# Moving the stationary operands of the split products to 64 bytes past a 128-byte line

## The chip, the cores and the metric

The kernel runs on one core of one Trainium2 chip. The metric is the device time of one execution in microseconds (us); the program is launched once and nothing else runs on the core. A difference of 0.3% is about 3.9 us here.

## What is computed

Four residual layers (a token mixer and a dense MLP each) over one sequence of 256 tokens with 1024 features, all in float32, and a last RMSNorm:

```python
for i in range(DEPTH):                       # DEPTH = 4, mixers: MLA, MoBA, SSD, MLA
    h = rmsnorm(x, norm_mix[i])
    m = mla_mixer(...) | moba_mixer(...) | ssd_mixer(...)
    x = x + m
    x = x + sq_relu_mlp(rmsnorm(x, norm_mlp[i]), mlp_w1[i], mlp_w2[i])
return rmsnorm(x, norm_final)

def sq_relu_mlp(h, w1, w2):                  # w1: 1024 x 4096, w2: 4096 x 1024
    a = jax.nn.relu(h @ w1)
    return (a * a) @ w2
```

The weights are some 220 MB in float32, read from memory once.

## The kernel before, in words

**Products in three parts.** A float32 product is made of three fast ones. Each operand is split into a high part in the type `float32r` and a low part (the rest), and high x high, high x low and low x high are added up in PSUM. `mm3` (L590, L591, L592) does it with 256 or 512 columns; in an MLP the first product is `pe_up` (L982: both halves of the input beside each other, 512 columns; L987: the low weights with 256 columns), and products back to the model width are `pe_out_part` (L902, L903, L906, 512 columns each). Each of these matmuls has its own weight load (LDWEIGHTS) of 128 columns, which is issued ahead, while the matmul before it streams. In the names of the profile's rows the moving operand stands first and the stationary one second: `bank<-hsplit,whi` streams the split input past weights, `bank<-whi,hsplit` and `acc<-whi,uhi` stream weights past a stationary input.

**Weights.** A unit of weights is up to 2048 columns in each of 128 partitions. Units pass through four slots: a DMA from the queue of SP fills `raw`, ScalarE (L557) writes the high part to `whi`, VectorE (L573) writes the rest to `wlo`, and TensorE frees the slot. Units run three ahead of their use. In an MLP a unit of `w1` (`up`) and one of `w2` (`down`) follow each other, 16 of each.

**The input.** The normed input is transposed on TensorE (L795) and split by ScalarE (L646) and VectorE (L723) into `hsplit`, hi and lo halves of 256 tokens for each of 8 feature blocks. Before the change this tensor is used under two layouts: `hsplit`, which begins 16 elements (64 bytes) into a row of 544 elements, in the mixers, and `hflat`, which begins at its first byte with rows of 512, in the MLPs. `split_input(j)` chooses.

**One MLP chunk** (`pe_mlp`, for c of 2 to 15): 24 matmuls of 512 columns for the `down` of two chunks ago, with the squares `uhi`/`ulo` stationary and weights moving; then `pe_up` of this chunk: 16 matmuls of 512 columns (L982) and 16 of 256 (L987), with the weights stationary and `hflat` moving. The mixers' outputs (`ohi`/`olo` of the heads, `ghi`/`glo` of SSD) go through the same `pe_out_part`.

**Order.** All engines' programs are written out by hand; semaphores couple them. PSUM has four accumulators (`acc`) and four banks in turn (`bank`), planned by `Jobs`.

Of the kernel before, what the change touches and what calls it, by code (L numbers as in the profile page):

```python
# [14 lines left out]
F32 = mybir.dt.float32  # L15
F32R = mybir.dt.float32r
# [5 lines left out]
P = 128  # L22
SEQ = 256
# [9 lines left out]
SLOTS = 4  # L33
UNIT = 2048
AHEAD = 3

# [66 lines left out]
def build(nc, A, out, stages):  # L103

    ctx = ExitStack()
    with ctx:
# [98 lines left out]
        with ExitStack() as stage:  # L205
            S_sb = sb("S_sb", [P, 2, 384], F32, stage)
            P_sb = sb("P_sb", [P, 2, 384], F32, stage)
            PT_sb = sb("PT_sb", [P, 2, 384], F32, stage)
            ohi = sb("ohi", [P, 2, 2, SEQ], F32R, stage)
            olo = sb("olo", [P, 2, 2, SEQ], F32R, stage)  # L210
            qT = sb("qT", [P, 2, 4, SEQ], F32, stage)
# [23 lines left out]
        with ExitStack() as stage:  # L235
# [12 lines left out]
            gss = sb("gss", [P, 512], F32, stage)  # L248
            ghi = sb("ghi", [P, 2, 2, SEQ], F32R, stage)
            glo = sb("glo", [P, 2, 2, SEQ], F32R, stage)  # L250
        acs_dram = nc.dram_tensor("acs_rows", (SSD_H, SEQ), F32, kind="Internal").ap()
# [23 lines left out]

        units, first = [], {}

        view = {}

        def unit(key, a, b, *srcs):  # L280

            first[key] = len(units)
            view[key] = (0, a, b)
            units.append((a, b, srcs))

        def unit_of_two(keys, shapes, srcs):

            off, parts = 0, []
            for key, (a, b), src in zip(keys, shapes, srcs):
# [254 lines left out]
        def act_splits(act, key, ahead=AHEAD):  # L544

            while split_to["act"] < min(first.get(key, key) + ahead + 1, len(units)):
# [4 lines left out]
                if k:  # L551
                    act.wait_ge(w_used[s], k)
                lo = 0
                if n in in_halves:
                    lo = e // 2
                    nc.scalar.activation(whi[:, s, :lo], raw[:, s, :lo], ACT.Copy).then_inc(half_hi_done, 1)
                nc.scalar.activation(whi[:, s, lo:e], raw[:, s, lo:e], ACT.Copy).then_inc(w_hi_done[s], 1)  # L557
                split_to["act"] += 1

        def dve_splits(dve, key, ahead=AHEAD):  # L560

            while split_to["dve"] < min(first.get(key, key) + ahead + 1, len(units)):
                n = split_to["dve"]
                s, k = n % SLOTS, n // SLOTS
                e = units[n][0] * units[n][1]
                lo = 0
                if n in in_halves:
                    lo = e // 2
                    dve.wait_ge(half_hi_done, n + 1)
                    nc.vector.tensor_tensor(wlo[:, s, :lo], raw[:, s, :lo], whi[:, s, :lo].bitcast(F32),  # L570
                                            ALU.subtract).then_inc(half_split, 1)
                dve.wait_ge(w_hi_done[s], k + 1)
                nc.vector.tensor_tensor(wlo[:, s, lo:e], raw[:, s, lo:e], whi[:, s, lo:e].bitcast(F32),  # L573
                                        ALU.subtract).then_inc(w_split[s], 1)
# [61 lines left out]

        def split_input(j):

            h = hflat if deferred(j) else hsplit
            return h[:, :, 0, :], h[:, :, 1, :]  # L640

        def act_tr(act, j, t):
            hhi, _ = split_input(j)
            for half in range(2):
# [74 lines left out]
        def dve_tr(dve, j, t, halves=(0, 1)):  # L719
            hhi, hlo = split_input(j)  # L720
            for half in halves:
# [119 lines left out]
        def pe_first_channels(te, j, keys):  # L841
# [5 lines left out]
            half = KD // 2  # L847
            hhi, hlo = split_input(j)

# [124 lines left out]
        def pe_up(te, L, c):  # L974
# [4 lines left out]
            for m in range(2):  # L979
                ps = open_job(te, key + (m,))  # L980
                for k in range(KD):
                    nc.tensor.matmul(ps, w[0][:, k, m * P:(m + 1) * P], hflat[:, k].rearrange("p a n -> p (a n)"),  # L982
                                     start=k == 0, stop=False)
            for m in range(2):
                ps = bank[jobs.at[key + (m,)][0]]
                for k in range(KD):
                    mm = nc.tensor.matmul(ps[:, 0:SEQ], w[1][:, k, m * P:(m + 1) * P], hflat[:, k, 0, :], start=False,  # L987
                                          stop=k == KD - 1)
# [1346 lines left out]
```

## Time and profile before

| | |
|---|---|
| time, median of 3 runs | 1313.64 us (1311.10 to 1315.05) |
| span of the profiled execution | 1312.0 us |
| TensorE busy (matmuls) | 1286.5 us, 98% of the span, 7578 records |
| VectorE, ScalarE busy | 891.4 us (68%), 671.6 us (51%) |
| granted clock of TensorE | 0.998 of 2.4 GHz |
| DMA | 231 MB, 54% of the 16 engines' time |

The span runs from the first to the last instruction of the profiled execution. A matmul's record reaches from its start to the modelled end of its pipeline (390 ns for 512 columns), so records overlap; what a matmul costs is the time from its start to the start of the next one, called its **step** here. It is read from the starts in the timeline: first and last start of a run of matmuls, divided by their number.

### The profile page before, as it was taken

Reading aid. Unit: us, or ns where it says so; the run is one execution under the profiler, and the core shown is the slowest. Engines: PE = TensorE matmul, PEld = TensorE weight load, DVE = VectorE, ACT = ScalarE, POOL = GpSimd, SP = SyncE. Lnnn points to the kernel's source line nnn. Section 1 sums busy time; section 2 is a strip of 40 time slices with the busy share of each in tenths; the row PEclk is TensorE's granted clock in tenths of the full one; section 3 lists DMA queues with packets and bytes.
Section 4 is the critical chain, followed back from the end, with each engine's and each line's share of the span. In section 5 each row is a group of like instructions: output and inputs, shape, how many; then the busy total and the mean of one; then the engine's idle time right before and its main releaser. Section 6 shows DMA issues by size and latency. Waiting matters only on the chain.

```text
span 1312.0 us, 18369 instructions
## 1 busy us (share of the span) xinstructions
PE 1286.5 (98%) x7578; PEld 1126.3 (86%) x7578; DVE 891.4 (68%) x1180; ACT 671.6 (51%) x861; POOL 43.5 (3%) x58
## 2 busy tenths in 40 slices
PE   6999999999999999999999999999999999999998
PEld 5888888888999888887999888888887888888886
DVE  5877666665666666666899886766667876666664
ACT  5555554444555454444776644544445645454442
POOL 3000000000000000000101110000000000000000
PEclk9999999999999999999999999999999999999999
DMA  9744465555845475545574643755554334565540
GB/s 289 143 168 148 141 232 201 193 192 161 233 149 180 132 254 192 192 165 160 181 222 141 203 149 119 249 191 192 191 180 140 117 130 130 168 231 193 192 161 32
DMA packets 146067, 230.93 MB, mean 176 GB/s; under 512 B 7683, under 2 KB 112429, under 8 KB 145984
## 3 DMA queue, kind: packets, MB, share of 16 engines
q1 hardware_dynamic: 143136, 221.66, 50.8%
q0 software_dynamic: 2848, 8.10, 2.9%
q8 instruction: 61, 1.00, 0.3%
q14 instruction: 22, 0.18, 0.0%
HBM read 227.08 MB, written 2.65 MB: 175 GB/s over the span
## 4 chain that ended last, share of the span: by engine, by line
PE 88%; DVE 7%; DMA 1%; issue 1%; ACT 1%; POOL 1%; SPq 0%; POOLq 0%; DVEq 0%; ACTq 0%
PE bank L982 15%; PE acc L902 12%; PE acc L903 12%; PE acc L906 12%; PE bank L987 8%; PE bank L590 7%; PE bank L591 7%; PE bank L592 7%; DVE wlo L573 2%; PE bank L1402 1%; PE bank L1105 1%; PE bank L795 1%; PE bank L1408 1%; PE bank L1090 1%; DMA raw<-in_mla_w_in 1%
## 5 line engine op out<-in xcount | busy, mean ns | idle before, releaser
L573 DVE TENSOR_TENSOR wlo<-raw,whi 128x2048 fp32r<-128x2048 f32 (+2 forms) x207 | 464.7, 2255 | 139.6 <-ACT whi L557 139.5
L557 ACT ACTIVATE whi<-raw 128x2048 fp32r<-128x2048 f32 (+2 forms) x207 | 386.8, 1879 | 45.8 <-PE acc L906 44.2
L982 PE MATMUL bank<-hsplit,whi 128*128 128x512 f32 x896 | 212.2, 389 | 0.0
L903 PE MATMUL acc<-wlo,uhi 128*128 128x512 f32 x512 | 200.1, 391 | 0.0
L902 PE MATMUL acc<-whi,uhi 128*128 128x512 f32 x512 | 199.6, 390 | 0.0
L982 PEld LDWEIGHTS bank<-hsplit,whi 128*128 128x128 f32 x896 | 168.2, 188 | 34.9
L906 PE MATMUL acc<-whi,ulo 128*128 128x512 f32 x512 | 159.2, 390 | 0.0
L590 PE MATMUL bank<-hsplit,whi 128*128 128x256 f32 (+2 forms) x540 | 154.5, 286 | 0.3 <-DVE xn L1980 0.3
L592 PE MATMUL bank<-hsplit,wlo 128*128 128x256 f32 (+2 forms) x540 | 151.4, 280 | 0.0
L591 PE MATMUL bank<-hsplit,whi 128*128 128x256 f32 (+2 forms) x540 | 151.4, 280 | 0.0
L1027 ACT ACTIVATE relu<-bank 128x512 f32<-128x512 f32 x56 | 33.5, 598 | 188.9 <-PE bank L987 188.9
L987 PEld LDWEIGHTS bank<-hsplit,wlo 128*128 128x128 f32 x896 | 114.9, 191 | 4.4
L987 PE MATMUL bank<-hsplit,wlo 128*128 128x256 f32 x896 | 116.2, 283 | 0.0
L906 PEld LDWEIGHTS acc<-whi,ulo 128*128 128x128 f32 x512 | 96.1, 188 | 20.4
L903 PEld LDWEIGHTS acc<-wlo,uhi 128*128 128x128 f32 x512 | 96.4, 188 | 18.2
L902 PEld LDWEIGHTS acc<-whi,uhi 128*128 128x128 f32 x512 | 96.4, 188 | 18.0
L1048 DVE TENSOR_TENSOR relu<-bank,relu 128x512 f32<-128x512 f32 x56 | 38.7, 691 | 96.0 <-ACT relu L1027 96.0
L590 PEld LDWEIGHTS bank<-hsplit,whi 128*128 128x128 f32 (+2 forms) x540 | 100.9, 187 | 1.7 <-issue 1.3
L591 PEld LDWEIGHTS bank<-hsplit,whi 128*128 128x128 f32 (+2 forms) x540 | 100.8, 187 | 0.9 <-issue 0.7
L592 PEld LDWEIGHTS bank<-hsplit,wlo 128*128 128x128 f32 (+2 forms) x540 | 100.7, 187 | 0.0
L1032 ACT ACTIVATE uhi<-rsq 128x512 fp32r<-128x512 f32 x64 | 40.5, 633 | 110.6 <-DVE rsq L1050 81.9
L1053 DVE TENSOR_TENSOR ulo<-rsq,uhi 128x512 fp32r<-128x512 f32 x64 | 44.3, 693 | 47.6 <-ACT uhi L1032 47.6
(252 smaller groups left out, 1813.4 us busy)
## 6 DMA issues: line engine op xcount, KB each, us to landing
raw<-in_mlp_w SPq DMA_DIRECT2D x128, 1024.0 KB, 5.5
raw<-in_ssd_w_in SPq DMA_DIRECT2D x18, 1024.0 KB, 5.4
raw<-in_mla_w_o SPq DMA_DIRECT2D x16, 1024.0 KB, 4.9
raw<-in_mla_w_ukv SPq DMA_DIRECT2D x8, 1024.0 KB, 5.8
raw<-in_moba_w_qkv SPq DMA_DIRECT2D x16, 512.0 KB, 5.3
raw<-in_ssd_w_out SPq DMA_DIRECT2D x8, 1024.0 KB, 4.9
raw<-in_mla_w_uq SPq DMA_DIRECT2D x8, 768.0 KB, 6.0
raw<-in_mla_w_in SPq DMA_DIRECT2D x4, 1024.0 KB, 7.5
```

What stands on the lines that cost most here:

```text
L557: nc.scalar.activation(whi[:, s, lo:e], raw[:, s, lo:e], ACT.Copy).then_inc(w_hi_done[s], 1)
L573: nc.vector.tensor_tensor(wlo[:, s, lo:e], raw[:, s, lo:e], whi[:, s, lo:e].bitcast(F32), ALU.subtract).then_inc(w_split[s], 1)
L590: nc.tensor.matmul(ps, lhs[0], rhs[0], start=start, stop=False)
L591: nc.tensor.matmul(ps, lhs[0], rhs[1], start=False, stop=False)
L592: return nc.tensor.matmul(ps, lhs[1], rhs[0], start=False, stop=stop)
L902: nc.tensor.matmul(acc[t][half][:], lh, wh[:, k, n], start=begin and k == 0, stop=False)
L903: nc.tensor.matmul(acc[t][half][:], lh, wl[:, k, n], start=False, stop=False)
L906: mm = nc.tensor.matmul(acc[t][half][:], ll, wh[:, k, n], start=False, stop=end and k == 1)
L982: nc.tensor.matmul(ps, w[0][:, k, m * P:(m + 1) * P], hflat[:, k].rearrange("p a n -> p (a n)"), start=k == 0, stop=False)
L987: mm = nc.tensor.matmul(ps[:, 0:SEQ], w[1][:, k, m * P:(m + 1) * P], hflat[:, k, 0, :], start=False, stop=k == KD - 1)
L1032: nc.scalar.activation(uhi[:, c % 2].rearrange("p a b -> p (a b)"), rsq[:, c % 2, :], ACT.Copy).then_inc(uhi_done, 1)
L1053: nc.vector.tensor_tensor(ulo[:, c % 2].rearrange("p a b -> p (a b)"), rsq[:, c % 2, :], uhi[:, c % 2].rearrange("p a b -> p (a b)").bitca ...
```

## The change

It moves addresses within the partitions, and nothing else: each engine issues the same instructions, with the same sizes and waits, in the same order. Where the operands of the three-part products start, in bytes modulo 128, in the programs as they are built:

| moving, stationary | matmuls | before | after |
|---|---|---|---|
| L982: `hsplit`, `whi` (512 columns) | 896 | 0, 0 | 0, 64 |
| L987: `hsplit`, `wlo` (256) | 896 | 0, 0 | 0, 64 |
| L902, L903, L906: `whi`/`wlo`, `uhi`/`ulo` (512) | 1536 | 0, 0 | 0, 64 |
| the same with `ohi`/`olo`, `ghi`/`glo` (512) | 672 | 0, 0 | 0, 64 |
| L590 to L592, L855 to L861: `hsplit`, weights, first two chunks of an MLP (256) | 384 | 0, 0 | 0, 64 |
| L590 to L592: `hsplit`, weights, in mixers (256) | 1248 | 64, 0 | 0, 64 |
| L590 to L592: `chi`/`clo`, weights of `uq` (256) | 192 | 0, 0 | 0, 64 |
| L590 to L592: weights of `mv`, `hsplit` (256) | 180 | 0, 64 | 64, 0 |
| L590 to L592, L1312 to L1318: weights of `ca`/`cb`, `hsplit` (512) | 84 | 0, 64 | 0, 0 |

`uq` is MLA's query weights, `mv` MoBA's value weights, `ca`/`cb` MLA's input weights. Each slot of `whi` and `wlo` grows by 128 bytes, to 8320, so that slots start in turn at 128 and 0 modulo 256. `hflat` and `split_input` go, and `hsplit` is one dense tensor at a 128-byte line.

```diff
+HALF_LINE = 16
-        whi = sb("whi", [P, SLOTS, UNIT], F32R)
-        wlo = sb("wlo", [P, SLOTS, UNIT], F32R)
+        whi = sb("whi", [P, SLOTS, UNIT + 2 * HALF_LINE], F32R)
+        wlo = sb("wlo", [P, SLOTS, UNIT + 2 * HALF_LINE], F32R)
-        hrows = sb("hsplit", [P, KD, 2 * SEQ + 32], F32R)
-        hsplit = hrows[:, :, 16:16 + 2 * SEQ].rearrange("p k (a n) -> p k a n", a=2)
-        hflat = hrows[:].rearrange("p k n -> p (k n)")[:, 0:KD * 2 * SEQ].rearrange("p (k a n) -> p k a n", k=KD, a=2)
+        hsplit = sb("hsplit", [P, KD, 2, SEQ], F32R)
-            uhi = sb("uhi", [P, 2, 2, SEQ], F32R, stage)
-            ulo = sb("ulo", [P, 2, 2, SEQ], F32R, stage)
+            uhi, ulo = (sb(n, [P, 2 * HALF_LINE + 4 * SEQ], F32R, stage)[:, HALF_LINE:-HALF_LINE].rearrange(
+                "p (b a n) -> p b a n", b=2, a=2) for n in ("uhi", "ulo"))
...
+        def start_of(kind):
+
+            if kind in ("ca", "cb", "down", "wo", "so", "ukv"):
+                return (0, 0)
+            return (HALF_LINE, HALF_LINE) if kind == "up" else (HALF_LINE, HALF_LINE)
+
         def unit(key, a, b, *srcs):
 
             first[key] = len(units)
+            starts.append(start_of(key if key == "dt" else key[0]))
...
             off, a, b = view[key]
             s = first[key] % SLOTS
-            return (whi[:, s, off:off + a * b].rearrange("p (a b) -> p a b", a=a),
-                    wlo[:, s, off:off + a * b].rearrange("p (a b) -> p a b", a=a))
+            hi, lo = (off + start for start in starts[first[key]])
+            return (whi[:, s, hi:hi + a * b].rearrange("p (a b) -> p a b", a=a),
+                    wlo[:, s, lo:lo + a * b].rearrange("p (a b) -> p a b", a=a))
...
-        def split_input(j):
-
-            h = hflat if deferred(j) else hsplit
-            return h[:, :, 0, :], h[:, :, 1, :]
-
...
                 for k in range(KD):
-                    nc.tensor.matmul(ps, w[0][:, k, m * P:(m + 1) * P], hflat[:, k].rearrange("p a n -> p (a n)"),
+                    nc.tensor.matmul(ps, w[0][:, k, m * P:(m + 1) * P], hsplit[:, k].rearrange("p a n -> p (a n)"),
                                      start=k == 0, stop=False)
```

`ohi`/`olo` and `ghi`/`glo` change as `uhi`/`ulo` do, and the splits on ScalarE and VectorE (L557, L573) write to the shifted places.

## Rows read from the trace of the kernel before

**Rows 1.** Page, parts 1 and 2: busy time by engine; granted clock in tenths
```profile
PE 1286.5 (98%) x7578; PEld 1126.3 (86%) x7578; DVE 891.4 (68%) x1180; ACT 671.6 (51%) x861; POOL 43.5 (3%) x58
PEclk9999999999999999999999999999999999999999
```

**Rows 2.** Page, part 4: the chain that ended last, by engine
```profile
PE 88%; DVE 7%; DMA 1%; issue 1%; ACT 1%; POOL 1%; SPq 0%; POOLq 0%; DVEq 0%; ACTq 0%
```

**Rows 3.** Waits of TensorE and VectorE: total us, times, longest us
```profile
PE bank L795 <- DVE xn L700: 8.9, 2, 8.0
PE acc L902 <- DVE wlo L573: 0.8, 2, 0.4
...
DVE wlo L573 <- ACT whi L557: 139.5, 136, 3.4
```

**Rows 4.** Timeline of TensorE, one MLP chunk: start us, us, engine, line
```profile
302.81 0.40 PE L902 MATMUL acc<-whi,uhi 128*128 128x512 f32 x1
...
308.28 3.79 PE L982 MATMUL bank<-hsplit,whi 128*128 128x512 f32 x16
311.91 2.08 PE L987 MATMUL bank<-hsplit,wlo 128*128 128x256 f32 x16
...
313.82 0.40 PE L902 MATMUL acc<-whi,uhi 128*128 128x512 f32 x1
```

**Rows 5.** Timeline, weights of `ca`/`cb` streaming past `hsplit`, fourth layer and first
```profile
992.28 0.40 PE L591 MATMUL bank<-wlo,hsplit 128*128 128x512 f32 x1
992.52 0.39 PE L592 MATMUL bank<-whi,hsplit 128*128 128x512 f32 x1
992.75 0.40 PE L590 MATMUL bank<-whi,hsplit 128*128 128x512 f32 x1
...
1000.41 0.28 PE L590 MATMUL bank<-hsplit,whi 128*64 128x256 f32 x1
...
26.16 0.40 PE L591 MATMUL bank<-wlo,hsplit 128*128 128x512 f32 x1
...
28.72 0.33 PE L590 MATMUL bank<-hsplit,whi 128*64 128x256 f32 x1
```

**Rows 6.** Timeline, weights of `mv` streaming past `hsplit` in MoBA
```profile
343.35 0.28 PE L592 MATMUL bank<-whi,hsplit 128*128 128x256 f32 x1
...
346.07 0.28 PE L592 MATMUL bank<-whi,hsplit 128*128 128x256 f32 x1
```

**Rows 7.** Timeline, `hsplit` streaming past weights in SSD, a mixer
```profile
648.83 0.28 PE L590 MATMUL bank<-hsplit,whi 128*128 128x256 f32 x1
...
652.01 0.28 PE L590 MATMUL bank<-hsplit,whi 128*128 128x256 f32 x1
```

**Rows 8.** Timeline, `hsplit` streaming past weights in an MLP's first two chunks
```profile
161.75 0.28 PE L590 MATMUL bank<-hsplit,whi 128*128 128x256 f32 x1
...
166.31 0.28 PE L592 MATMUL bank<-hsplit,wlo 128*128 128x256 f32 x1
```

**Rows 9.** Timeline, one step of a mixer's output product among attention's matmuls
```profile
138.57 0.39 PE L903 MATMUL acc<-wlo,ohi 128*128 128x512 f32 x1
...
141.11 0.59 PE L1105 MATMUL bank<-PT_sb,v_sb 128*128 128x256 f32 x2
141.54 0.27 PE L1106 MATMUL bank<-PT_sb,v_sb 128*128 128x128 f32 x1
```

**Rows 10.** Windows: us, then busy (instructions) of PE, PEld, DVE, ACT, POOL; PEclk, DMA share, GB/s
```profile
302.82:313.82 11.00, 11.00 (x58) 9.42 (x57) 6.66 (x5) 4.96 (x4) 0.00 (x0) 1.00 0.56 186
992.28:1000.41 8.13, 8.13 (x37) 6.52 (x35) 6.16 (x6) 6.54 (x9) 0.70 (x1) 1.00 0.28 79
343.35:346.07 2.72, 2.72 (x27) 2.72 (x25) 1.72 (x2) 2.72 (x2) 0.00 (x0) 1.00 1.04 355
```

**Rows 11.** The line of VectorE's half of the input split: min/median/max ns, forms
```profile
L723 DVE TENSOR_TENSOR hsplit<-bank,hsplit x32: 679/688/693, 9.7 to 1132.0; 128x512 fp32r<-128x512 f32 x32
```

More of the change, by code:

```diff
@@ L208, in build @@
             PT_sb = sb("PT_sb", [P, 2, 384], F32, stage)
-            ohi = sb("ohi", [P, 2, 2, SEQ], F32R, stage)
-            olo = sb("olo", [P, 2, 2, SEQ], F32R, stage)
+            ohi, olo = (sb(n, [P, 2 * HALF_LINE + 4 * SEQ], F32R, stage)[:, HALF_LINE:-HALF_LINE].rearrange(
+                "p (b a n) -> p b a n", b=2, a=2) for n in ("ohi", "olo"))
             qT = sb("qT", [P, 2, 4, SEQ], F32, stage)
@@ L248, in build @@
             gss = sb("gss", [P, 512], F32, stage)
-            ghi = sb("ghi", [P, 2, 2, SEQ], F32R, stage)
-            glo = sb("glo", [P, 2, 2, SEQ], F32R, stage)
+            ghi, glo = (sb(n, [P, 2 * HALF_LINE + 4 * SEQ], F32R, stage)[:, HALF_LINE:-HALF_LINE].rearrange(
+                "p (b a n) -> p b a n", b=2, a=2) for n in ("ghi", "glo"))
         acs_dram = nc.dram_tensor("acs_rows", (SSD_H, SEQ), F32, kind="Internal").ap()
@@ L276, in build @@
         units, first = [], {}
+        starts = []
         view = {}
+        def start_of(kind):
+            if kind in ("ca", "cb", "down", "wo", "so", "ukv"):
+                return (0, 0)
+            return (HALF_LINE, HALF_LINE) if kind == "up" else (HALF_LINE, HALF_LINE)
         def unit(key, a, b, *srcs):
             first[key] = len(units)
+            starts.append(start_of(key if key == "dt" else key[0]))
             view[key] = (0, a, b)
@@ L288, in unit_of_two @@
             off, parts = 0, []
+            starts.append(start_of(keys[0][0]))
             for key, (a, b), src in zip(keys, shapes, srcs):
@@ L552, in act_splits @@
                     act.wait_ge(w_used[s], k)
-                lo = 0
+                lo, high = 0, whi[:, s, starts[n][0]:starts[n][0] + e]
                 if n in in_halves:
                     lo = e // 2
-                    nc.scalar.activation(whi[:, s, :lo], raw[:, s, :lo], ACT.Copy).then_inc(half_hi_done, 1)
-                nc.scalar.activation(whi[:, s, lo:e], raw[:, s, lo:e], ACT.Copy).then_inc(w_hi_done[s], 1)
+                    nc.scalar.activation(high[:, :lo], raw[:, s, :lo], ACT.Copy).then_inc(half_hi_done, 1)
+                nc.scalar.activation(high[:, lo:e], raw[:, s, lo:e], ACT.Copy).then_inc(w_hi_done[s], 1)
                 split_to["act"] += 1
@@ L565, in dve_splits @@
                 e = units[n][0] * units[n][1]
-                lo = 0
+                lo, high, low = 0, whi[:, s, starts[n][0]:starts[n][0] + e], wlo[:, s, starts[n][1]:starts[n][1] + e]
                 if n in in_halves:
@@ L569, in dve_splits @@
                     dve.wait_ge(half_hi_done, n + 1)
-                    nc.vector.tensor_tensor(wlo[:, s, :lo], raw[:, s, :lo], whi[:, s, :lo].bitcast(F32),
+                    nc.vector.tensor_tensor(low[:, :lo], raw[:, s, :lo], high[:, :lo].bitcast(F32),
                                             ALU.subtract).then_inc(half_split, 1)
                 dve.wait_ge(w_hi_done[s], k + 1)
-                nc.vector.tensor_tensor(wlo[:, s, lo:e], raw[:, s, lo:e], whi[:, s, lo:e].bitcast(F32),
+                nc.vector.tensor_tensor(low[:, lo:e], raw[:, s, lo:e], high[:, lo:e].bitcast(F32),
                                         ALU.subtract).then_inc(w_split[s], 1)
@@ L719, in dve_tr @@
         def dve_tr(dve, j, t, halves=(0, 1)):
-            hhi, hlo = split_input(j)
             for half in halves:
@@ L986, in pe_up @@
                 for k in range(KD):
-                    mm = nc.tensor.matmul(ps[:, 0:SEQ], w[1][:, k, m * P:(m + 1) * P], hflat[:, k, 0, :], start=False,
+                    mm = nc.tensor.matmul(ps[:, 0:SEQ], w[1][:, k, m * P:(m + 1) * P], hsplit[:, k, 0, :], start=False,
                                           stop=k == KD - 1)
```

2 lines of the change are left out of this document (removed).

## The prediction, made before the run

> **What bounds the kernel now.** I read the busy shares first: TensorE has work in flight for 98% of the span, at a granted clock of nine tenths or more in every slice; VectorE is at 68%, ScalarE at 51% [rows 1]. The chain that ended last is 88% TensorE [rows 2], and TensorE waits for little: 8.9 us in all for the normed input, 0.8 us for split weights [rows 3]. VectorE waits 139.5 us for ScalarE's half of the weight split, so the splitting engines have slack. The end is set by TensorE's own steps, and what counts is how long a matmul of 256 or 512 columns holds the engine until the next may start.
>
> So the next view is the timeline, read for steps. At 2.4 GHz, 512 columns stream in 213.3 ns and 256 in 106.7 ns. One MLP chunk [rows 4]: 24 `down` matmuls from 302.81 to 308.28 us are 227.9 ns each; the 16 of L982 from 308.28 to 311.91 are 226.9; the 16 of L987 from 311.91 to 313.82 are 119.4. The clock in that window is 1.00 of full [rows 10], so 13 ns a matmul are neither the stream nor a slow clock. Since VectorE is busy for only 6.66 of these 11.00 us and TensorE never pauses, it is not a wait for another engine either. What runs beside a stream is the next weight load.
>
> **What alignment does, as far as this trace shows it.** The trace of before holds three of the four combinations of (moving, stationary) modulo 128:
> - (0, 0): the MLP chunk, 227 ns and 119.4 ns [rows 4]; with 256 columns also the first two chunks of an MLP, 38 steps from 161.75 to 166.31 us, 120.0 ns each [rows 8].
> - (64, 0), 256 columns: the mixers' products, 27 steps from 648.83 to 652.01 us, 117.8 ns [rows 7].
> - (0, 64), which the change makes the rule. 256 columns: MoBA's `mv`, 24 steps from 343.35 to 346.07, 113.3 ns [rows 6]. 512 columns: MLA's `ca`/`cb` in the fourth layer, 35 steps from 992.28 to 1000.41, 232.3 ns, and in the first, 11 steps from 26.16 to 28.72, 232.7 ns [rows 5].
>
> So the same shift shortens a 256-column step by 6 ns and lengthens a 512-column step by 5. The 512-column steps were not slowed by waits: no row of the stretch has one, and the clock is 1.00 [rows 10]. Nor do they settle: 232.3 is a mean over steps that move around it (240 and 230 are the first two [rows 5]), where the 512-column steps of the MLP stand still at 226.9. I read it so: with 256 columns the weight load (128 columns at half the rate) is as long as the stream and sets the step, and a load from a shifted place isn't held up; with 512 columns the load is over in half the step, and it is the stream that pays for the meeting, a little more when the two lie 64 bytes apart.
>
> The Trainium skill speaks against any effect at all. By its page "SBUF — State Buffer", section "Who interferes with whom", TensorE has two independent read ports, one for the moving operand and one for LDWEIGHTS, and never waits on anyone; by that rule the sum would be 0. The steps above, which differ by 6.7 ns with nothing but the address changed, do not agree with it.
>
> **The sum**, against the span of 1312.0 us; the median of the runs is 1.6 us above it:
> - L982, 896 x (232.3 - 226.9) = +4.8 us.
> - `down` of the MLPs, 1536 matmuls from 227.9 to 232.3: +6.8 us.
> - `wo` and `so`, 672 matmuls. Among attention's matmuls they come in short runs whose steps are already 230.9 ns (11 from 138.57 to 141.11 us [rows 9]), in long ones as in the MLP: between 672 x 1.4 = +0.9 and 672 x 4.4 = +3.0; I take +2.0, the middle, as the trace has both kinds.
> - L987, 896 x (113.3 - 119.4) = -5.5 us.
> - First two chunks of the MLPs, 384 x (113.3 - 120.0) = -2.6 us.
> - Mixers' products, 1248 x (113.3 - 117.8) = -5.6 us; the first step behind a wait is not shortened, and I take -5.0.
> - `uq`'s 192 with `chi`, which is (0, 0) now: -1.3 us.
> - `mv`, the other way round: 180 x (117.8 - 113.3) = +0.8 us. `ca`/`cb` go to (0, 0): 84 x (227 - 232.3) = -0.4 us.
> - The splits and evictions write 64 bytes off. L723 does so before the change in the mixers and not in the MLPs, and takes 679 to 693 ns over both [rows 11]: 0, and what it took would be hidden behind TensorE's work. In the mixers TensorE gets 4% faster; the weights come three units ahead and waited-for splits are 0.8 us [rows 3], so I let nothing new become late.
>
> The three terms of 512 columns give +13.6 us, those of 256 give -13.6, `ca`/`cb` -0.4: **-0.4 us**, a span of 1311.6 and a time of 1313.64 - 0.4 = 1313.2, call it 1313.5 for the stretches where a step beside a wait keeps its length. It is a small difference of two large terms: 1 ns in the step of the 3104 wide matmuls is 3.1 us. The samples of that step are 46, in two layers; 231 to 233.5 is as far as I trust them, which is -4 to +4 us.
>
> **Rivals.**
> 1. *The wide steps stay as they are.* In every wide run of before, the step becomes steady at 226.9. The samples of (0, 64) alternate between stationary tiles at 64 and 192 modulo 256 from one feature block to the next; in L982 after the change, a whole run keeps one of them, and could settle. Then only the narrow terms are left: -14 us, 1299.7 us. Against it: within the samples, three matmuls in a row with the same place don't settle. Half of it (L982 alone, or only some slots) would be 1305 to 1309.
> 2. *The streams meet no load any more.* If 64 bytes apart were the cure in wide products too, the step would come near the stream. The nearest row is the float32 product of L1105, two records of 215 ns [rows 9]: 3104 x (215 - 227.6) = -39 us on top of -14, 1261 us. The samples at 232 speak against it. The Trainium skill ("TensorE: Matmul & The Clock Gate", section "Back-to-back issue gap") gives 518 cycles at N=512 and 262 at N=256, an estimate of 216 and 109 ns; by it all steps of before are 6 to 10 ns too long, and the sum would be some -36 us for the wide ones alone. No stretch of fast products in this trace reaches those.
> 3. *Slower: a steady slow step.* The same settling, but at a longer step. The wide products after the change see streams at 128 and at 0 modulo 256 (slots of 8320 bytes), the samples only 128. The first steps in the samples reach 240 ns; at a steady 236 the wide terms are +26 us against -14, so 1325.5 us. It decides from 233.6 ns on: 3104 x 1.3 ns is the 3.9 us that make 0.3%.
> 4. *The addresses don't matter*, and the differences come from what else goes on in those stretches. Then the time is 1313.6. The 256-column steps of 113.3 with DMA at 1.04 of its engines and both splitters at work [rows 10] speak against it; it isn't told apart from my forecast by the time, but by the steps.
>
> **How the numbers follow.** My forecast (wide 231 to 233.5, narrow 113.3) gets 0.50, rival 1 with its halves 0.23, rival 2 0.06, rival 3 0.17, rival 4 0.04. A change within 0.3% (3.9 us) is about what a measurement of this kernel can't tell from none. Same: nearly all of the forecast (0.43) and rival 4, with 0.02 from light forms of the others: 0.49. Faster: rivals 1 and 2, and the forecast's low end: 0.32. Slower: rival 3 and the high end: 0.19. The range has to take in rival 1 whole (1299.7, with 2 us for the bounds of its narrow terms: 1297.5) and most of rival 3 (to a wide step of 234.7, 1321); outside are rival 2 and the worst of rival 3, some 0.12, and a little at both ends. The forecast's own range is 1309.5 to 1317.5.
>
> **What the profile after would show.** Right: L987's 16 steps in 1.81 us instead of 1.91, and the mixers' steps at 113.3 in place of 117.8, while L982's 16 take 3.72 us instead of 3.63 and do not stand still; the chunk stays at about 11.0 us. Wrong, to the fast side: L982's 16 in 3.63 us or less. Wrong, to the slow side: a wide step above 233.6, most likely in the slots that start at 0 modulo 256, or a wait of TensorE for `wlo` in the mixers, where VectorE is now asked for units 4% sooner. What would upset the whole working is a narrow step that isn't 113.3 outside MoBA: the only samples of it have the input stationary and the weights moving, and the change has it the other way round.

## The result, and the profile after

The kernel after takes 1322.53 us, the median of 4 runs (1318.5 to 1323.55); the kernel before took 1314.35 us beside it (1311.1 to 1315.71). The ratio is 1.0063, 95% interval [1.0043, 1.0083]. The change makes the kernel slower by some 8 us. The forecast was no change (1313.5 us), and the measured time lies above the range's upper end of 1321.0. Two of ten executions of u_up_shifted (1424.17 and 5673.52 us) and one of the kernel before beside the last two experiments (1363.52 us) ran over 1.5% above the fastest of their kernel and are left out of all comparisons.

The page of one execution of the kernel after, which took 1318.5 us, the fastest of the four; parts 1, 2 and 4:

```profile
span 1316.7 us, 18369 instructions
PE 1289.6 (98%) x7578; PEld 1116.2 (85%) x7578; DVE 891.2 (68%) x1180; ACT 672.0 (51%) x861; POOL 43.5 (3%) x58
PEclk9999999999999999999999999999999999999999
PE 84%; DVE 11%; ACT 2%; issue 1%; DMA 1%; POOL 0%; SPq 0%; POOLq 0%; DVEq 0%; ACTq 0%
```

Little here looks different from [rows 1]: the same instructions, the same busy shares, the same clock. TensorE's busy time is 3.1 us longer. The chain is still TensorE's, 84% where it was 88% [rows 2], with VectorE at 11% where it was 7%. Waits are few, as in [rows 3], with one that is new, the first `down` product of each MLP for VectorE's squares:

```profile
PE bank L797 <- DVE xn L703: 8.6, 2, 7.5
PE acc L903 <- DVE ulo L1054: 0.9, 4, 0.2
PE acc L903 <- DVE wlo L582: 0.8, 2, 0.4
DVE wlo L582 <- ACT whi L566: 144.4, 136, 3.4
```

So the loss must be in the steps. The timeline of TensorE in the kernel after, read as [rows 4] was, one MLP chunk of the first MLP and one of the third (start us, us, engine, line; L983 is what was L982, L988 was L987, L903 was L902):

```profile
177.91 3.83 PE L983 MATMUL bank<-hsplit,whi 128*128 128x512 f32 x16
181.57 1.98 PE L988 MATMUL bank<-hsplit,wlo 128*128 128x256 f32 x16
183.38 0.39 PE L903 MATMUL acc<-whi,uhi 128*128 128x512 f32 x1
...
188.97 3.83 PE L983 MATMUL bank<-hsplit,whi 128*128 128x512 f32 x16
...
850.14 3.89 PE L983 MATMUL bank<-hsplit,whi 128*128 128x512 f32 x16
853.88 1.98 PE L988 MATMUL bank<-hsplit,wlo 128*128 128x256 f32 x16
855.70 0.40 PE L903 MATMUL acc<-whi,uhi 128*128 128x512 f32 x1
...
861.25 3.90 PE L983 MATMUL bank<-hsplit,whi 128*128 128x512 f32 x16
```

In the first MLP L983 steps at 3.66 / 16 = 229 ns (the single steps go round 232, 226 and 229) and L988 at 1.81 / 16 = 113 ns; in the third at 3.74 / 16 = 234 and 1.82 / 16 = 114 ns. `down` takes 5.59 / 24 = 233 ns there and 5.55 / 24 = 231 here. The chunk, 11.01 us before, is 11.06 and 11.11 us. The clock is not in it; the window view of both chunks (us; busy of PE, PEld, DVE, ACT, POOL; PEclk, DMA share, GB/s) has it at 1.00, as in [rows 10]:

```profile
177.91:188.97 11.06, 11.06 (x58) 9.33 (x57) 7.70 (x7) 7.03 (x6) 0.00 (x0) 1.00 0.88 303
850.14:861.25 11.11, 11.11 (x57) 9.34 (x56) 6.67 (x6) 4.96 (x4) 0.00 (x0) 1.00 0.55 189
```

The mixers did not do what was forecast. Two stretches of SSD in the kernel after, 46 steps each, with `hsplit` streaming past weights as in [rows 7]:

```profile
708.58 0.28 PE L600 MATMUL bank<-hsplit,whi 128*128 128x256 f32 x1
...
713.79 0.28 PE L601 MATMUL bank<-hsplit,wlo 128*128 128x256 f32 x1
...
737.94 0.28 PE L600 MATMUL bank<-hsplit,whi 128*128 128x256 f32 x1
...
743.36 0.28 PE L601 MATMUL bank<-hsplit,wlo 128*128 128x256 f32 x1
```

The first makes its 46 steps in 5.21 us, 113.3 ns each, the second in 5.42 us, 117.8 each. Both have the weights 64 bytes off the line. Every long stretch of MoBA's and SSD's products takes one of the two values or a mix of them.

Matching the two traces matmul by matmul (7578 in each) and adding up the differences of their steps gives the whole sum, in us, against the forecast's terms. Steps that differ by over 60 ns stand by themselves, as "beside their waits". The last column is a second profiled execution of the same kernel (a_again, below), since one execution is not the median:

| term | forecast | kernel after | after, again |
|---|---|---|---|
| L982 (L983), 896 | +4.8 | +4.0 | +5.0 |
| `down`, 1536 | +6.8 | +6.8 | +7.0 |
| `wo`, `so`, 672 | +2.0 | +2.3 | +2.3 |
| L987 (L988), 896 | -5.5 | -5.3 | -4.3 |
| first two chunks, 384 | -2.6 | -2.4 | -2.4 |
| ... steps beside their waits | 0 | +1.6 | +1.6 |
| mixers' products | -5.0 | -1.3 | -1.4 |
| ... steps beside their waits | 0 | -1.3 | -0.2 |
| `uq` | -1.3 | -0.7 | -0.7 |
| `mv`, `ca`/`cb`, `ukv` | +0.4 | +1.2 | +1.5 |
| all else | 0 | +0.2 | -0.2 |
| sum | -0.4 | +5.1 | +8.1 |

The spans differ by 4.7 and 7.8 us (1312.0, 1316.7, 1319.8); the rest lies before the first matmul.

### The profile page after: what moved, and what is told of

Read it like the earlier page. It is cut to its first block, busy times and chain, and to the rows that moved or that the text cites. A ratio compares the mean times of both kernels' runs of the same rounds, so it can differ in the third digit from the quotient of the medians.

```text
span 1316.7 us, 18369 instructions
## 1 busy us (share of the span) xinstructions
PE 1289.6 (98%) x7578; PEld 1116.2 (85%) x7578; DVE 891.2 (68%) x1180; ACT 672.0 (51%) x861; POOL 43.5 (3%) x58
## 4 chain that ended last, share of the span: by engine, by line
PE 84%; DVE 11%; ACT 2%; issue 1%; DMA 1%; POOL 0%; SPq 0%; POOLq 0%; DVEq 0%; ACTq 0%
PE bank L983 16%; PE acc L903 13%; PE acc L907 13%; PE acc L904 13%; PE bank L988 8%; PE bank L599 5%; PE bank L601 4%; PE bank L600 4%; DVE wlo L582 4%; DVE cacc L1951 2%; PE bank L1403 1%; PE bank L1106 1%; ACT whi L566 1%; PE bank L797 1%; PE bank L1409 1%
## 5 line engine op out<-in xcount | busy, mean ns | idle before, releaser
L983 PE MATMUL bank<-hsplit,whi 128*128 128x512 f32 x896 | 216.2, 393 | 0.0
L903 PE MATMUL acc<-whi,uhi 128*128 128x512 f32 x512 | 202.3, 395 | 0.9 <-DVE ulo L1054 0.9
L983 PEld LDWEIGHTS bank<-hsplit,whi 128*128 128x128 f32 x896 | 168.3, 188 | 39.0
L903 PEld LDWEIGHTS acc<-whi,uhi 128*128 128x128 f32 x512 | 96.2, 188 | 21.8 <-DVE ulo L1054 1.7
L988 PEld LDWEIGHTS bank<-hsplit,wlo 128*128 128x128 f32 x896 | 110.2, 188 | 5.0
L988 PE MATMUL bank<-hsplit,wlo 128*128 128x256 f32 x896 | 110.9, 276 | 0.0
L1054 DVE TENSOR_TENSOR ulo<-rsq,uhi 128x512 fp32r<-128x512 f32 x64 | 44.3, 692 | 47.8 <-ACT uhi L1033 47.8
```

The source lines that it names most:

```text
L903: nc.tensor.matmul(acc[t][half][:], lh, wh[:, k, n], start=begin and k == 0, stop=False)
L983: nc.tensor.matmul(ps, w[0][:, k, m * P:(m + 1) * P], hsplit[:, k].rearrange("p a n -> p (a n)"), start=k == 0, stop=False)
L1054: nc.vector.tensor_tensor(ulo[:, c % 2].rearrange("p a b -> p (a b)"), rsq[:, c % 2, :], uhi[:, c % 2].rearrange("p a b -> p (a b)").bitca ...
```

## The experiments

In what follows the *distance* is the place of the stationary tile less the place of the streamed one, modulo 256 bytes. In the kernel before, the slots of the split weights are 8192 bytes apart, and every product of 512 columns in the MLPs, `wo` and `so` has distance 0. The change makes a slot 8320 bytes long, so slots alternate between two halves of 256 bytes, and distances become 64 and 192. All `up` chunks of one MLP lie in slots of one kind: in the first two MLPs L983 has distance 192, in the last two 64. The squares' two halves `uhi` and `ulo` are 4224 bytes apart, so that a run of `down` changes between 64 and 192 in every MLP. The kernel before beside the experiments took 1313.78 to 1315.10 us in the median.

**The change again.** a_again: no edit.

> The changed kernel once more, for its spread and a second profile. Before this run: its profiled execution had a span of 1316.7 us, its other executions 1320.6 to 1321.8, and a median of 1322.5 against 1314.4. If the executions differ because a run of narrow matmuls may settle at one of two steps (113.3 or 117.8 ns), the second profile has another mix of the two in the mixers and a span that goes with it: each 100 matmuls that fall the other way are 0.45 us. If they differ by short drops of TensorE's clock, as between 10 and 40 us in the first profile (0.94 of full), the mix stays and the windows' clock differs. Time 1318 to 1324 either way.

Measured: 1321.59 us (6 runs, 1319.56 to 1322.86), ratio 1.0058 [1.0046, 1.0070]. The timeline of its first MLP:

```profile
176.76 3.90 PE L983 MATMUL bank<-hsplit,whi 128*128 128x512 f32 x16
180.50 2.04 PE L988 MATMUL bank<-hsplit,wlo 128*128 128x256 f32 x16
182.38 0.39 PE L903 MATMUL acc<-whi,uhi 128*128 128x512 f32 x1
...
187.98 3.90 PE L983 MATMUL bank<-hsplit,whi 128*128 128x512 f32 x16
```

The same program and addresses, at 3.74 / 16 = 234 ns and 1.88 / 16 = 118, where the execution above has 229 and 113. It is so for all 14 chunks of that MLP; the second MLP, at the same distance, is at 229 and 113 in both executions, the last two at 233 and 114 in both. The mixers have another mix, as the first theory has it: eight of SSD's twelve stretches of 48 products or more stand at another value than in the first execution (one of 48 products at 113.7 ns there and 117.9 here), yet their sum is the same, -1.3 and -1.4 us. The clock is no answer: between 10 and 40 us it is 0.94 in both. A chunk takes 11.22 us in place of 11.06; over 14 chunks that is some 2 us for each MLP that takes the slower pattern. This is one part of why the profiled execution of 1318.5 us was the fastest: two runs of the kernel after, both at a mean granted clock of 0.998, took 1318.5 and 1323.55 us.

**Only the narrow products shifted.** b_narrow_only: `up`'s hi weights, squares, heads and gated outputs go back to their line.

```
-            return (HALF_LINE, HALF_LINE) if kind == "up" else (HALF_LINE, HALF_LINE)
+            return (0, HALF_LINE) if kind == "up" else (HALF_LINE, HALF_LINE)
-  ... F32R, stage)[:, HALF_LINE:-HALF_LINE]      (uhi/ulo, ohi/olo, ghi/glo)
+  ... F32R, stage)[:, 0:4 * SEQ]
```

> The changed kernel with the wide products taken back to (0, 0) modulo 128: whi of up, and the squares, heads and gated outputs, start at their line; wlo of up and all narrow products stay shifted; slots stay 8320 bytes. If only the place modulo 128 counts, wide steps are back at 226.9 ns and the kernel loses the 12 us that the wide steps cost: about 1310 us, below before. Rival: the place modulo 256 counts too. The slots begin at 128 and at 0 in turn, and the profile of the changed kernel shows 229 ns for L983 with weights at 64 modulo 256 and 233 with weights at 192; then half of the wide steps, those whose operands are 128 apart modulo 256, stay near 233 ns and the kernel ends at about 1316 us.

Measured: 1324.13 us (4 runs), ratio 1.0079 [1.0064, 1.0095]. This is above both theories, 1310 and 1316 us. Putting the wide operands back to their lines gains nothing: L983 averages 231.1 ns (232.9 at distance 128, 229.3 at 0) and `down`, which changes between 0 and 128, 233.1, as slow as when shifted or slower. A line of 128 bytes is not the unit in which places count.

**No shift at all, only the longer slot.** p_pad_alone: the kernel after, with every start at 0 (as above, and `return (0, 0)` for all kinds), slots still 8320 bytes. The input keeps its new layout too, so that the mixers' products lie at 0 and 128.

> The kernel after with every 64-byte shift taken out again (split weights, squares, head and gated outputs start at their line), but with the weight slots still 8320 bytes apart instead of 8192. So every operand of a product lies at a 128-byte line, and what the two operands' places differ by is 0 or 128 bytes modulo 256, by the slot. Theory (the wide step depends on the two places' difference modulo 256, and 0 alone gives the steady 226.7 ns): L983 stays near 227 to 230 ns in the two MLPs whose up slots lie at difference 0 and goes to 232 to 234 in the other two, the down products go to some 232 to 233 ns; +4 for L983, +8.5 for down, +1.5 for wo and so, and the mixers' narrow steps at 118 to 120: 1327 to 1330 us. Rival, the forecast's own picture (only the place within a 128-byte line counts): all wide steps 227, all narrow 120: 1313.8 + 2.8 for the mixers = 1316.5 us.

Measured: 1330.51 us (1329.33 to 1334.78, 4 runs), ratio 1.0129 [1.0107, 1.0152], just above the 1327 to 1330 us of the theory of 256 bytes and 14 us above its rival. All operands lie on a 128-byte line, and it is the slowest kernel of all. Its timeline, first MLP (distance 128) and third (distance 0):

```profile
176.35 3.89 PE L983 MATMUL bank<-hsplit,whi 128*128 128x512 f32 x16
180.08 2.05 PE L988 MATMUL bank<-hsplit,wlo 128*128 128x256 f32 x16
...
869.48 3.84 PE L983 MATMUL bank<-hsplit,whi 128*128 128x512 f32 x16
873.15 2.08 PE L988 MATMUL bank<-hsplit,wlo 128*128 128x256 f32 x16
```

3.73 / 16 = 233 ns at distance 128. At distance 0 it is 3.67 / 16 = 229, not the 227 of before: the first chunk of that MLP is at 227 and the 13 after it at 230. In these 13 only the first nine steps move about (224 to 236 ns); the last seven are 226 or 227, as before. All stand behind `down` products that change between distances 0 and 128, but the steps of the first such run follow another pattern than those of the later ones. Matched with before, the wide products lose 4.2 + 8.5 + 2.4 us here. The padding, which the change needs only to make room for the 16 elements, costs these products 15 us, more than the 13.6 us that the narrow terms were to bring.

**Wide at distance 0 again, narrow shifted.** e_narrow_256: as b_narrow_only, and in every other slot all line-aligned weights start 128 bytes later, so that the longer slot is made up for; the lo halves of squares, heads and gated outputs get the same 128 bytes.

```
+            whole = 2 * HALF_LINE * (len(units) % 2)
             if kind in ("ca", "cb", "down", "wo", "so", "ukv"):
-                return (0, 0)
+                return (whole, whole)
+            return (whole, HALF_LINE) if kind == "up" else (HALF_LINE, HALF_LINE)
```

> As the kernel before in this list, but every moving weight, the high part of up and the squares, heads and gated outputs are put at 128 modulo 256, where hsplit lies, by starting 128 bytes later in every second slot. Narrow products stay 64 bytes off. Both theories, modulo 128 and modulo 256, give wide steps of 226.9 ns; narrow ones are 113.4 (L988) and 113.3 to 117.8 in the mixers. Against before: -5.3 us for L988, -3 to -5 for the mixers, about -1 for the first two chunks, some of which is given back as a wait for ulo: 1305 us, 1303 to 1308. If the time comes out at or above 1314, shorter narrow steps are given back somewhere.

Measured: 1312.25 us (12 runs, 1310.38 to 1314.12), ratio 0.9987 [0.9978, 0.9996]. The loss is gone, all of it, with the longer slots still in place. The gain expected beside it is not there. First MLP:

```profile
176.80 3.79 PE L984 MATMUL bank<-hsplit,whi 128*128 128x512 f32 x16
180.43 2.05 PE L989 MATMUL bank<-hsplit,wlo 128*128 128x256 f32 x16
182.31 0.40 PE L904 MATMUL acc<-whi,uhi 128*128 128x512 f32 x1
```

L984 is back at 3.63 / 16 = 227 ns. But the narrow products, at the very places where the kernel after has 113, are at 1.88 / 16 = 118 in all 56 chunks. So a narrow step is not set by its own two places alone. The 1.5 us that L989 brings against the kernel before (117.8 in place of 119.5) are matched by 1.4 that `down` loses.

**Other distances.** s_sweep: `up`'s weights start 0, 16, ... 128 bytes into their slot, another in each chunk; the squares start elsewhere in each MLP.

> One look at many places in one kernel. In each MLP, up's high and low parts start 0, 16, 32 ... 128 bytes into their slot, another one in each chunk from the third on (so the distance from hsplit is 0 to 128 bytes in two MLPs, and 128 to 256 in the other two), and the squares start 32, 96, 192 and 128 bytes off their line in MLP 0, 1, 2, 3, with moving weights always at 128 modulo 256. If the distance modulo 128 were all that counts, the steps of the same offset agree in all MLPs and distance 128 gives 226.9 ns as 0 does. If it is modulo 256, L983 gives 226.9 at distance 0 and 256 alone, about 233 at 64 and 128 and 229 at 192. If only 64-byte halves count, distances of 16, 32 and 48 bytes give what 0 gives. The narrow L988 has 113.3 ns at a distance of 64 and 192 and 120 at 0; between, unknown. Time not predicted beyond 1310 to 1325.

Measured: a single run, 1322.44 us. First MLP, its chunks at distance 192 and at 0 (the fifth and the ninth of the 14):

```profile
222.50 3.84 PE L989 MATMUL bank<-hsplit,whi 128*128 128x512 f32 x16
226.17 1.98 PE L994 MATMUL bank<-hsplit,wlo 128*128 128x256 f32 x16
227.99 0.40 PE L909 MATMUL acc<-whi,uhi 128*128 128x512 f32 x1
...
267.12 3.79 PE L989 MATMUL bank<-hsplit,whi 128*128 128x512 f32 x16
270.75 2.07 PE L994 MATMUL bank<-hsplit,wlo 128*128 128x256 f32 x16
```

Start to start over 16, for all chunks, in ns:

| distance | 0 | 16 | 32 | 48 | 64 | 80 | 96 | 112 |
|---|---|---|---|---|---|---|---|---|
| wide | 227-229 | 227, 233 | 233 | 233 | 233 | 232 | 234 | 233 |
| narrow | 120 | 118 | 118 | 118 | 114 | 119 | 118 | 120 |

| distance | 128 | 144 | 160 | 176 | 192 | 208 | 224 | 240 |
|---|---|---|---|---|---|---|---|---|
| wide | 232-233 | 233 | 233-234 | 229-231 | 229-230 | 232-233 | 233 | 228-229 |
| narrow | 118-120 | 119-120 | 120 | 118 | 114, 118 | 117 | 117 | 117 |

`down`'s step by the distance of its MLP, the first step of each run left out: 32 bytes 233.2, 96 bytes 234.1, 128 bytes 232.6, 192 bytes 229.1. Apart from 16 bytes, only 0 gives 227. Distances 0 and 128 differ, and so do 64 (233) and 192 (229), which a count modulo 128 can't have. At 16 bytes the third MLP has 233 in both of its chunks and the fourth 227 in both, again two patterns at one place. These two MLPs differ in the place of their squares, so the `down` products before each chunk may be what decides; no run separates that.

**Distance or place?** h_input_128: the split input, and all behind it, moved by 128 bytes. The padding of `ghi` and `glo` is also cut by 64 bytes each, so that SSD's `glo` moves by 64 only; the MLPs don't use it.

```
-        hsplit = sb("hsplit", [P, KD, 2, SEQ], F32R)
+        hsplit = sb("hsplit", [P, 32 + KD * 2 * SEQ], F32R)[:, 32:].rearrange(...)
```

> The kernel after with the split input (and with it all that lies behind it) 128 bytes further on; the weight slots stay where they are. If the difference of the two places counts, the two pairs of MLPs change roles: L983 goes from 228.9 to 233 ns in the first and third and from 233.1 to 229 in the second and fourth. If it is the place of the stationary weights alone, each MLP keeps its step (228.9, 233.1, 228.9, 233.1). The time stays within 3 us of the kernel after by both.

Measured: a single run, 1324.44 us. (The pairs that change roles are the first two MLPs and the last two, not as the expectation has them.) First MLP, then third:

```profile
178.24 3.89 PE L983 MATMUL bank<-hsplit,whi 128*128 128x512 f32 x16
181.97 1.98 PE L988 MATMUL bank<-hsplit,wlo 128*128 128x256 f32 x16
...
864.93 3.90 PE L983 MATMUL bank<-hsplit,whi 128*128 128x512 f32 x16
868.67 2.04 PE L988 MATMUL bank<-hsplit,wlo 128*128 128x256 f32 x16
```

The first two MLPs, now at distance 64, went from 229 to 3.73 / 16 = 233 ns with the weights in the same place, and their steps repeat the 231 and 236 ns of distance 64 in the kernel after. That is what the distance asks, and speaks against the place. The last two, now at distance 192, should have come down to 229; they stayed at 234 with narrow steps of 118, the slower pattern of a_again's first MLP. Half of what was expected came.

**Up shifted alone.** u_up_shifted: e_narrow_256 with `up`'s weights at distances 192 and 64 as in the kernel after (`return (HALF_LINE, HALF_LINE)`).

> The kernel after with its down, wo and so products back at equal places modulo 256 (moving weights and stationary squares, heads and gated outputs); up's split weights keep their shift, so L983 and L988 stand as in the kernel after. Theory: the products whose moving operand are the weights carry the greater part of the loss, 6.8 + 2.4 us, so the time is 9 us under the kernel after, 1312.5 us, and L983's own loss (+4.1 us) is made up by the narrow steps. Rival (the pieces hang together: a steady state in down is what lets L983 and L988 settle): L983 leaves 229.1 and 233.2 ns for another pair, and the time is not the sum, under 1310 or over 1316 us.

Measured: 1317.08 us (8 runs), ratio 1.0016 [1.0002, 1.0030]. L984 is at 228.9 and 233.3 ns as in the kernel after, `down` at 228.2. But L989 is at 117.8 and 117.9 ns in the two kinds of MLP, where the kernel after has 113.3 and 113.9: the time is not the sum. The rival was right on the time and in that the pieces hang together, but it is the narrow step that left its value, not L984. Against before it is +4.0 for the wide `up` products and only -1.5 for the narrow ones. In the kernel after the -5.3 comes together with `down`'s +6.8.

**What a run is entered from.** f_wide_split cuts the last wide product of each chunk of e_narrow_256 into two of 256 columns; f_narrow_split cuts the first narrow one into two of 128.

```
+                    last = (m, k) == (1, KD - 1)
+                    for a in ((0, 1), (1, 2)) if last else ((0, 2),):
+                        nc.tensor.matmul(ps[:, a[0] * SEQ:a[1] * SEQ], w[0][:, k, m * P:(m + 1) * P], ...
...
+                    cuts = (0, P, SEQ) if (m, k) == (0, 0) else (0, SEQ)
```

> The kernel of e_narrow_256 (wide operands at equal places modulo 256, narrow ones 64 bytes apart) with the last wide product of each MLP chunk split into two of 256 columns, so that the 16 narrow products are entered from another step. Theory (the narrow step has two settled values, 113.3 and 117.8 ns, and what it was entered from decides which): the 16 steps fall to 113.3 ns, -4.0 us in 56 chunks, against +0.6 us for the split: 1309 us. Rival (a narrow step entered beside steady wide ones at an equal place is 117.8 for another reason, as DMA or the splitting engines in that stretch): they stay at 117.8 and the time is 1313 us.

> The kernel of e_narrow_256 with the first narrow product of each MLP chunk split into two of 128 columns, one weight load more. Theory of the two settled values: if the entry decides, the following 15 steps may fall to 113.3 ns (-3.8 us in 56 chunks), against some +3 us for the added product: 1311 to 1312 us, and if it enters at the same value, 117.8 and 1315 us. Rival (the entry doesn't matter): 117.8 ns and 1315 us.

Measured: 1311.98 us (12 runs), ratio 0.9981 [0.9969, 0.9992], with the 16 narrow steps still at 117.8; and 1317.06 us (10 runs), ratio 1.0016 [1.0003, 1.0030], where the run begins with longer steps (over the 14 steps behind the cut the mean is 122 ns at distance 192 and 119 at 64, the figures that the next expectation quotes) and then settles at 117.8 in the first two MLPs, distance 192, and at 113.3 in the last two, distance 64, in place of 117.8. The first cut changed nothing, the second did in half of the chunks. So the entry matters, and the question was which entry. v_entry_sweep cuts elsewhere in each chunk:

```
+   cuts = (0, 32 * (c - 1), 2 * SEQ) if L < 2 and (m, k) == (1, KD - 1) else (0, 2 * SEQ)     (wide)
+   cuts = (0, 16 * (c - 1), SEQ) if L > 1 and (m, k) == (0, 0) else (0, SEQ)                  (narrow)
```

> The kernel of e_narrow_256 with another entry into the 16 narrow products in each of the 14 chunks of an MLP: in the first two MLPs the last wide product is cut in two at column 32, 64, ... 448, in the last two the first narrow product at column 16, 32, ... 224. All places stay the same. Theory (what a run of narrow products is entered from decides at which step it settles): the 56 runs settle at two or more different steps, 113.3 among them at some cuts, each steady through its run. Rival (places and neighbours alone decide): the runs of one MLP all settle at the same step, 117.8, or the 122 and 119 that an added narrow product gave. The time is not of interest, some 3 to 8 us above e_narrow_256.

Measured: a single run, 1312.51 us. The chunks whose last wide product is cut at column 160, and at 192:

```profile
218.25 3.83 PE L986 MATMUL bank<-hsplit,whi 128*128 128x512 f32 x17
221.92 2.04 PE L994 MATMUL bank<-hsplit,wlo 128*128 128x256 f32 x16
223.80 0.40 PE L904 MATMUL acc<-whi,uhi 128*128 128x512 f32 x1
...
229.25 3.82 PE L986 MATMUL bank<-hsplit,whi 128*128 128x512 f32 x17
232.91 1.98 PE L994 MATMUL bank<-hsplit,wlo 128*128 128x256 f32 x16
234.73 0.40 PE L904 MATMUL acc<-whi,uhi 128*128 128x512 f32 x1
```

1.88 / 16 = 118 ns after the one, 1.82 / 16 = 114 (113.3 once settled) after the other, with the same two operands. In both of the first two MLPs the cuts at 128, 192 and 416 lead to 113.3 and the other eleven to 117.8. In the last two, where the first narrow product is cut, the value goes by turns: the seven cuts at a multiple of 32 columns settle at 113.3, after some longer steps, and the seven at an odd multiple of 16 at 117.8, in both MLPs alike. The last 11 products of the chunks cut at 32 and at 48:

```profile
839.51 1.42 PE L994 MATMUL bank<-hsplit,wlo 128*128 128x256 f32 x11
840.76 0.40 PE L904 MATMUL acc<-whi,uhi 128*128 128x512 f32 x1
...
850.54 1.46 PE L994 MATMUL bank<-hsplit,wlo 128*128 128x256 f32 x11
851.84 0.39 PE L904 MATMUL acc<-whi,uhi 128*128 128x512 f32 x1
```

The first block takes 1.25 us, 113.6 ns each, the second 1.30 us, 118.2 each. So at these distances a run of narrow steps has two values it can hold, and what it is entered from decides which. As the cut goes by the chunk here, the chunk itself could be the cause; against it stands the next kernel, where the cut at 192 leads to 113.3 in all 14 chunks of these two MLPs.

**A better version.** z_cut_192 takes e_narrow_256 with that cut in every chunk; z_first_chunks also shifts both halves of the weights in each MLP's first two chunks.

> The kernel of e_narrow_256 with the last wide product of each MLP chunk cut at column 192, the cut after which v_entry_sweep's narrow products settled at 113.3 ns at the least cost (86 + 174 ns in place of 227). Theory: +33 ns for the cut and 16 x 4.5 = 72 ns less for the narrow steps, 39 ns in each of 56 chunks, -2.2 us against e_narrow_256: 1310 us, ratio to the kernel before 0.997. Rival (the gain comes back as a wait of the down products): the steps fall to 113.3 ns and the time stays at 1312 us.

> z_cut_192 with the split weights of each MLP's first two chunks 64 bytes further on, as in the kernel after: 384 narrow products, in e_narrow_256 at 117 to 119 ns, in the kernel after at 113.4. Theory: they fall to 113.4 ns, up to 1.7 us, but the first down product waits for VectorE's squares all the same, so that the wait before it grows by as much: no change, 1310 us. Rival: the gain stays, 1308.5 us.

Measured: 1311.69 us (12 runs), ratio 0.9977 [0.9966, 0.9988], and 1311.79 us (10 runs), ratio 0.9978 [0.9964, 0.9993]. Faster than both kernels, by 0.2% against before, but less than expected, and not told apart by the time from e_narrow_256 (0.9987 [0.9978, 0.9996]). The cut gives 113.3 in 28 of 56 chunks and 117.8 in the other 28, all those of the last two MLPs, whose narrow products lie at distance 64. The sweep had cut the wide product only in the first two, at distance 192. The cut costs 28 to 33 ns in each chunk, 1.7 us in all, and the shorter steps bring 72 ns in half of them, 2.0 us. z_cut_192, first MLP and third:

```profile
177.76 3.82 PE L987 MATMUL bank<-hsplit,whi 128*128 128x512 f32 x17
181.42 1.98 PE L993 MATMUL bank<-hsplit,wlo 128*128 128x256 f32 x16
183.23 0.40 PE L904 MATMUL acc<-whi,uhi 128*128 128x512 f32 x1
...
870.49 3.82 PE L987 MATMUL bank<-hsplit,whi 128*128 128x512 f32 x17
874.14 2.05 PE L993 MATMUL bank<-hsplit,wlo 128*128 128x256 f32 x16
876.02 0.40 PE L904 MATMUL acc<-whi,uhi 128*128 128x512 f32 x1
```

In z_first_chunks a wait stands that z_cut_192 doesn't have, and that the kernel after has:

```profile
PE acc L906 <- DVE ulo L1061: 0.9, 4, 0.2
```

The first two chunks run faster and the `down` product behind them then waits for VectorE's squares: what is won there is given back, and the time is the same.

## Why the prediction was wrong

**What held.** The loss is in TensorE's steps, and the three wide terms were +13.6 us in the forecast, +13.1 and +14.2 in the two executions. L987 and the first two chunks came at -5.3 (-4.3 in the second execution) and -2.4, where -5.5 and -2.6 were forecast. The splits didn't get late (L903 for `wlo`: 0.8 us, as before), and VectorE's L725 takes 687 ns, as [rows 11]. By the Trainium skill's page "SBUF — State Buffer", section "Who interferes with whom", TensorE's two read ports are independent and it never waits on anyone. The kernels here don't agree with that: p_pad_alone and e_narrow_256 differ in nothing but addresses, and by 18 us (1.0129 and 0.9987 of the kernel before beside each).

**The step that failed is the mixers' term, 1248 x (113.3 - 117.8).** Both its ends were read from one stretch each. Over all of them the step was 117.2 before (stretches of 116.7 and of 117.7) and is 116.1 after (113.3 and 117.8 side by side): -1.3 us, not -5.0, and that is 3.7 us of the miss. The deeper mistake is in the table under "what alignment does": three classes of (moving, stationary) modulo 128. By distance modulo 256 the mixers before stood at 64 and 192 already, where the change leaves them; it only takes the shift from one operand and gives it to the other. What it changes is the order: before, 64 and 192 took turns from one feature block to the next, since the input's rows were 2176 bytes long, and after it a whole unit of weights keeps one of them. MoBA's 113.3 [rows 6] was at the same distances as the mixers' 117.8 [rows 7]. The forecast saw two numbers for what is one case with two settled values and made them two cases. It also says that nothing but the address differed between its narrow samples, and that isn't so: in MoBA's rows the weights stream, in the others the input. The prediction's last sentence had named this, a narrow step that isn't 113.3 outside MoBA, and given it no place in the range.

**Work taken off the first two chunks came back.** The forecast let -2.6 us stand because no wait was near. The squares of the first chunk were due just then: +1.6 us in the steps beside the waits, and among them the wait for `ulo` L1054, 0.9 us in four. z_first_chunks against z_cut_192 shows the same.

**`uq`, `mv`, `ca`/`cb` and `ukv`** account for another 1.5 us. `uq` came to 115.8 ns (114.2 in the first layer, 117.3 in the fourth), not the 113.3 that the same class gave it. In the rest the added time is the granted clock's: in the first layer four 512-column steps of `ukv`, from 35.2 us on, take 426 ns in place of some 227 and a fifth 559 in place of 319, and two of 256 columns are lengthened too, 1.3 us in all. At 1.2 GHz, the lower of the clock's two levels, 512 columns are 427 ns. Over the stretch from 10 to 40 us the granted clock is 0.94 in this execution and was 1.00 in that of before:

```profile
10.00:40.00 30.00, 25.12 (x125) 19.02 (x125) 20.06 (x43) 17.76 (x30) 9.73 (x13) 0.94 0.91 295
```

The kernel before lost a like piece between 600 and 630 us, at 0.94, where the kernel after is at 1.00: ten of SSD's narrow products took 213 ns each there. They are 1.0 of the mixers' -1.3 us "beside their waits", so the two pieces nearly cancel.

**One execution stood for the median.** The sum was set against a profiled run; but the change makes the wide step at distance 192 one with two patterns, 229 with 113 behind it or 233 with 118, 2 us for each MLP. The profiled execution had both such MLPs in the faster one (+4.7 us of span), a_again's one of two (+7.8). The median, +8, lies with the latter.

**The rivals.** Rival 1 (wide stays at 226.9) and rival 2 fell. Rival 3, a steady slow step, was right on the side and nearly on the time (1325.5), but by another way than its words: over both executions the wide step averages 231.8 to 232.2 ns, under its threshold of 233.6; the missing microseconds are in the narrow terms. That the time came near is luck. Its remark that slots of 8320 bytes bring a place the samples didn't have was the right thread: the samples had both 64 and 192 mixed in each run, and their mean of 232.3 hides two cases. Rival 4 fell with the steps. In rival 2 the steps of before are said to be 6 to 10 ns over the two estimates there, 216 and 109 ns; the steps that the prediction reads, 226.9 to 227.9 and 113.3 to 120.0, are 4 to 12 over. Nothing else hangs on it.

**What stays open.** Why distance 0 gives 227 and its neighbour 16 sometimes 233; why a cut at a multiple of 32 columns leads to the shorter step and one 16 columns on does not; what carries a pattern through the `down` products from chunk to chunk, so that an MLP keeps it for 14 chunks; and what decides it at the MLP's start. No run here took that apart.

## What to carry to other kernels

When two operands' relative place matters, take the period from the data, not from a round number: padding a ring of buffers by 128 bytes moved every other slot and cost 15 us in wide steps, more than the shift it served could bring. Keep the operands of long runs of wide matmuls at equal places modulo 256 bytes, by starting every other slot 128 bytes later, as e_narrow_256 does; padding by a multiple of 256 should do the same and was not run. And where a step can settle at more than one value, read it over all stretches and from two executions before multiplying it by a thousand.

## What the runs showed of the hardware that was not expected

- A matmul of 512 float32r columns settles at 226.7 ns in the MLPs of every kernel here in which the stationary tile and the streamed one lie at equal places modulo 256 bytes, at once or after some longer steps. At 32 to 160 bytes' distance it is 232 to 234 ns, at 176 and 192 bytes 229 to 231 or 233, at 208 and 224 again 232 to 233, at 240 it is 228 to 229, and at 16 it was 227 in one MLP and 233 in another.
- A run of 256-column matmuls at distance 64 or 192 holds 113.3 or 117.8 ns, by what stood before it: the column at which the preceding matmul is cut decides, in the same way in two MLPs. Of fourteen cuts in the last wide product, at distance 192, three lead to 113.3; of fourteen in the first narrow one, at distance 64, the seven at a multiple of 32 columns.
- The same program at the same addresses can run an MLP's 14 chunks at 229 and 113 ns in one execution and at 233 and 118 in the next, with the granted clock at 1.00 in both.
- Of the eight kernels with the same products, the one with every operand at a 128-byte line is the slowest (1330.5 us), and one whose wide operands lie at such lines too, but at equal places modulo 256, the fastest (1312.3 us).
